# Even stage unrolled over heads, with chunk scores and turned keys computed once, decay rows brought by DMA, and four attention weights loaded into buffers of their own

## The reference

```python
b = lax.cumsum(fc, axis=2)
d = jnp.where(lower, b[..., :, None] - b[..., None, :] + ic[..., None, :], -jnp.inf)
inter = b + m_st[..., None]
m_t = jnp.maximum(inter, jnp.max(d, axis=-1))
w = jnp.exp(d - m_t[..., None])
a_inter = jnp.exp(inter - m_t)
s = jnp.einsum('bhtd,bhsd->bhts', qc, kc) * w
num = jnp.einsum('bhts,bhsd->bhtd', s, vc) + a_inter[..., None] * jnp.einsum('bhtk,bhkd->bhtd', qc, c_st)
den = jnp.sum(s, axis=-1) + a_inter * jnp.einsum('bhtk,bhk->bht', qc, n_st)
h = num / jnp.maximum(jnp.abs(den), jnp.exp(-m_t))[..., None]
...
kw = kc * w_tok[..., None]
c_new = decay[..., None, None] * c_st + jnp.einsum('bhsk,bhsd->bhkd', kw, vc)
n_new = decay[..., None] * n_st + jnp.sum(kw, axis=2)
```

## Time and profile before

| | us |
|---|---|
| median of 3 runs | 3407.57 (3403.55 to 3410.09) |
| the profiled execution | 3409.28 |
| its span, first to last instruction | 3407.5 |
| PE busy | 3097.1 (91%) |
| DVE busy | 1566.3 (46%) |
| ACT busy | 1215.2 (36%) |

### The profile page before, as it was taken

The page is one execution under the profiler, slowest core; times in us unless marked ns, Lnnn a source line. Parts: engine busy times, 40 slices in busy tenths (PEclk is TensorE's granted clock), DMA queues, the critical chain, the costliest instruction groups (busy, mean ns, idle before and its releaser), DMA issues. The chain is left out here.

```text
span 3407.5 us, 42438 instructions
## 1 busy us (share of the span) xinstructions
PE 3097.1 (91%) x16797; PEld 2659.2 (78%) x16797; DVE 1566.3 (46%) x2651; ACT 1215.2 (36%) x1967; POOL 102.1 (3%) x118
## 2 busy tenths in 40 slices
PE   5547999999999999999799799699999999999798
PEld 4436898888888888888678578588888888888577
DVE  3352354235424542454444332265665665665443
ACT  2331222122212221222221432166666666665400
POOL 0000000000000000000023000000000000000000
PEclk7768999999999999999899899899999999999899
DMA  5401111111111101110533323100000000000431
GB/s 186 148 26 39 32 33 33 49 31 33 33 54 32 33 27 54 31 33 29 211 100 104 127 68 99 54 23 22 26 29 29 26 29 31 18 29 19 161 99 62
DMA packets 217411, 196.27 MB, mean 58 GB/s; under 512 B 10350, under 2 KB 191998, under 8 KB 217218
## 3 DMA queue, kind: packets, MB, share of 16 engines
q1 hardware_dynamic: 200916, 166.82, 15.5%
q0 software_dynamic: 5904, 21.50, 1.7%
q10 hardware_dynamic: 10400, 5.24, 0.5%
HBM read 152.62 MB, written 40.91 MB: 57 GB/s over the span
## 5 line engine op out<-in xcount | busy, mean ns | idle before, releaser
L40 PE MATMUL v_pj<-e_u_hi,v_w_hi 128*128 128x512 f32 (+1 forms) x1728 | 624.4, 361 | 18.8 <-issue 9.7
L41 PE MATMUL v_pj<-e_u_lo,v_w_hi 128*128 128x512 f32 (+1 forms) x1728 | 620.7, 359 | 0.9 <-issue 0.9
L42 PE MATMUL v_pj<-e_u_hi,v_w_lo 128*128 128x512 f32 (+1 forms) x1728 | 620.6, 359 | 0.0
L40 PEld LDWEIGHTS v_pj<-e_u_hi,v_w_hi 128*128 128x128 f32 x1728 | 329.8, 191 | 66.7 <-issue 19.6
L42 PEld LDWEIGHTS v_pj<-e_u_hi,v_w_lo 128*128 128x128 f32 x1728 | 329.3, 191 | 52.3 <-issue 1.1
L41 PEld LDWEIGHTS v_pj<-e_u_lo,v_w_hi 128*128 128x128 f32 x1728 | 329.7, 191 | 46.9
L40 PE MATMUL o_y_bank<-o_w_hi,o_m_hi 128*128 128x512 f32 x576 | 230.8, 401 | 48.0 <-DVE o_w_lo L1083 31.2
L1670 ACT CAST t_pt_hi<-t_ring 128x512 fp32r<-128x512 f32 (+1 forms) x384 | 181.3, 517 | 253.7 <-PE t_ring L1853 253.7
L41 PE MATMUL o_y_bank<-o_w_lo,o_m_hi 128*128 128x512 f32 x576 | 228.9, 397 | 0.0
L42 PE MATMUL o_y_bank<-o_w_hi,o_m_lo 128*128 128x512 f32 x576 | 228.7, 397 | 0.0
L1768 DVE TENSOR_REDUCE t_bias<-t_scores 128x1 f32<-128x1280 f32 x128 | 190.8, 1490 | 81.2 <-PE t_scores L1879 80.6
(11 more groups left out here) (335 smaller groups left out, 6093.5 us busy)
## 6 DMA issues: line engine op xcount, KB each, us to landing
v_w_raw<-in_ev_w_in SPq DMA_DIRECT2D x73, 512.0 KB, 3.8
m_w_raw<-in_mod_w SPq DMA_DIRECT2D x24, 1024.0 KB, 5.7
l_w_raw<-in_od_w_in SPq DMA_DIRECT2D x21, 512.0 KB, 3.8
o_m_raw<-mixT SPq DMA_DIRECT2D x20, 512.0 KB, 4.8
mixT<-v_buf SPq DMA_DIRECT2D x16, 512.0 KB, 2.7
o_w_raw<-in_ev_w_out SPq DMA_DIRECT2D x16, 512.0 KB, 9.5
zgT<-l_lat_q POOLq DMA_DIRECT2D x16, 512.0 KB, 3.4
t_zg<-zgT SPq DMA_DIRECT2D x32, 256.0 KB, 2.7
```

The source lines that it names most:

```text
L40: nc.tensor.matmul(out, whi, xhi, start=first, stop=False)
L41: nc.tensor.matmul(out, whi, xlo, start=False, stop=False)
L42: return nc.tensor.matmul(out, wlo, xhi, start=False, stop=last)
```

## The change

`stage_gates` writes the R rows of all heads and directions to a small tensor in memory. `stage_even` loses its loops: every engine's program is written out for 4 heads of 18 tiles. The scores and the turned keys of a chunk are made once for both directions, between the projections of tiles 4 and 5 (`prepare`), and VectorE copies them into SBUF over the halves of k. The decay rows come by a DMA that spreads a row over 128 partitions, two steps ahead, and GpSimd adds the mask. Z takes v with its column of ones (258 columns), so Y_n and its four short matmuls go. The waits are split: Y, Z and X have semaphores of their own. The convolution weights of all heads are loaded at once at the start of the stage. In `stage_attend` the first four weight loads have four buffers, laid over a tensor that is written later, and are issued one after the other without waiting.

```diff
+            sp.wait_ge(logf, 6)
+            for d in range(2):
+                sp.dma_start(a["r_rows"][4 * d:4 * d + 4, :], rows2("R")[32 * d:32 * d + 4, :]).then_inc(row_out, 16)
+            sp.wait_ge(row_out, 32)
...
+    PREPARED = {(4, 0): (0, 1), (4, 1): (2, 3), (4, 2): (4, 5), (5, 0): (6, 7), (5, 2): (8, 9)}
...
+        k_tok = over(nc, "v_k_tok", [P, 2, NT, P], F32, k_hi_at)
+        s_all = over(nc, "v_s_all", [P, NT, P], F32, k_lo_at)
...
+        wgt = [[s.sb(f"wgt{d}{x}", [P, P]) for x in range(2)] for d in range(2)]
...
+        Z = z_bank[:, :].rearrange("p (j c) -> p j c", c=512)[:, :, 0:HD + 2]
+        prep_bank = lambda c: e_bank[:, :] if c % 2 == 0 else z_half[1]
...
+            def load_row(h, n, d):
+                c = chunk(n, d)
+                old = step_at[(h, n, d)] - 4
+                if old > 0:
+                    sp.wait_ge(sw_ok, old)
+                row = a["r_rows"][4 * d + h:4 * d + h + 1, c * P:c * P + P]
+                sp.dma_start(wgt[d][n % 2][:, :], row.partition_broadcast(P)).then_inc(rows_in[d][n % 2], 16)
...
+            sp.dma_start(conv_w[:, :, :], a["conv_t"].rearrange("(m p) w -> p m w", p=P)).then_inc(cw_in, 16)
+            for d in range(2):
+                for n in range(2):
+                    load_row(0, n, d)
+            for h, t in tiles:
+                if tile_no[(h, t)] + 1 < len(tiles):
+                    load_w(*tiles[tile_no[(h, t)] + 1])
+                n = step_of(t)
+                if n is not None:
+                    nxt = (h, n + 2) if n + 2 < NT else (h + 1, n + 2 - NT)
+                    if nxt[0] < HEADS:
+                        for d in range(2):
+                            load_row(*nxt, d)
+                if t == 10:
+                    store(h, 1, 2 * h, (gate_part, gate_at[(h, 9, 2)]))
+                if t == 14:
+                    store(h, 1, 2 * h + 1, (gate_part, gate_at[(h, 13, 2)]))
+                if t == NTILE - 1:
+                    for j in range(2):
+                        store(h, j, KD + 2 * h + j, (ht_used, ht_at[(h, j, 2)]))
+            sp.wait_ge(mix_out, 32 * len(stores))
...
+        def _(pool):
+            pool.wait_ge(const_ok, 1)
+            for h, n, d in steps:
+                x = n % 2
+                pool.wait_ge(rows_in[d][x], 16 * (h * (NT // 2) + n // 2 + 1))
+                pool.tensor_tensor(wgt[d][x][:, :], wgt[d][x][:, :], mask[:, d, :], ALU.add).then_inc(masked, 1)
...
+                act.wait_ge(masked, g)
+                wg = wgt[d][n % 2]
+                nc.scalar.activation(wg[:, :], wg[:, :], ACT.Exp, bias=gate_col[:, 0, c, col:col + 1]).then_inc(wgt_ok, 1)
+                act.wait_ge(prep_ok, prep_at[(h, NT - 1)])
+                if g > 2:
+                    act.wait_ge(x_done, g - 2)
+                nc.scalar.mul(kw[d][0][:, :].rearrange("p (j e) -> p j e", e=P), k_tok[:, :, c, :], gate_col[:, 3, c, col:col + 1]).then_inc(kw_hi_ok, 1)
...
+            def prepared(h, c):
+                dve.wait_ge(prep_done, prep_at[(h, c)])
+                bank = prep_bank(c)
+                nc.vector.tensor_copy(s_all[:, c, :], bank[:, 0:P])
+                nc.vector.tensor_copy(k_tok[:, :, c, :], bank[:, P:3 * P].rearrange("p (j e) -> p j e", e=P)).then_inc(prep_ok, 1)
...
+                nc.vector.tensor_tensor(wg[:, :], s_all[:, c, :], wg[:, :], ALU.mult).then_inc(sw_f_ok, 1)
-                nc.vector.tensor_tensor(wgt[d][:, :], sek[d][:, 0:P], wgt[d][:, :], ALU.mult).then_inc(sw_f_ok, 1)
-                nc.vector.scalar_tensor_tensor(kw[d][1][:, :], sek[d][:, 2 * P:4 * P], hc[:, 3, c, d:d + 1], f(kw[d][0][:, :]),
+                parts = lambda ap: ap.rearrange("p (j e) -> p j e", e=P)
+                nc.vector.scalar_tensor_tensor(parts(kw[d][1][:, :]), k_tok[:, :, c, :], gate_col[:, 3, c, col:col + 1], parts(f(kw[d][0][:, :])),
...
+                    dve.wait_ge(z_done, with_state[st])
-                        nc.vector.tensor_copy(c_f32[d][:, :, HD:HD + 2], Y_n)
-                        nc.vector.tensor_copy(c_f32[d][:, :, 0:HD], Z).then_inc(c_f_ok, 1)
+                        nc.vector.tensor_copy(c_f32[d][:, :, :], Z).then_inc(c_f_ok, 1)
-                        dve.wait_ge(inter_ok, i * (NSTEP - 2) + 2 * (n - 1) + d + 1)
-                        for dst, new in ((slice(HD, HD + 2), Y_n), (slice(0, HD), Z)):
-                            last = nc.vector.scalar_tensor_tensor(c_f32[d][:, :, dst], c_f32[d][:, :, dst], hc[:, 5, c, d:d + 1],
-                                                                  new, ALU.mult, ALU.add)
-                        last.then_inc(c_f_ok, 1)
-                else:
-                    dve.wait_ge(inter_ok, i * (NSTEP - 2) + 2 * (n - 1) + d + 1)
+                        nc.vector.scalar_tensor_tensor(c_f32[d][:, :, :], c_f32[d][:, :, :], gate_col[:, 5, c, col:col + 1],
+                                                       Z, ALU.mult, ALU.add).then_inc(c_f_ok, 1)
...
-            def scores(i, n, d):
-                c = n if d == 0 else BWD[n]
-                t0 = c * P
-                if n == 0:
-                    pe.wait_ge(ht_used, i * 6 + 1)
-                    pe.wait_ge(pj_free_d, i * (3 * len(D_TILES)) + 13)
-                pe.wait_ge(diag_ok, i * NSTEP + 2 * n + d + 1)
-                bank = sek[d]
+            def prepare(h, c):
+                t0, bank = c * P, prep_bank(c)
+                pe.wait_ge(pj_free_d, dve_free[(h, 3, group_of(c))])
+                if c >= 2:
+                    pe.wait_ge(prep_ok, prep_at[(h, c - 2)])
+                elif h:
+                    pe.wait_ge(ht_used, ht_at[(h - 1, 1, 2)])
-                nc.tensor.matmul(bank[:, P:2 * P], ones[:, :], diag[d][:, :], start=True, stop=False)
-                nc.tensor.matmul(bank[:, P:2 * P], ident_b[:, :], mask[:, d, :], start=False, stop=True)
-                    nc.tensor.matmul(bank[:, (2 + j) * P:(3 + j) * P], k_hi[:, j, t0:t0 + P], ident_r[:, :], start=True, stop=False)
-                    last = nc.tensor.matmul(bank[:, (2 + j) * P:(3 + j) * P], k_lo[:, j, t0:t0 + P], ident_r[:, :], start=False, stop=True)
-                last.then_inc(sc_done, 1)
-            def state(i, n, d):
-                c, g = (n if d == 0 else BWD[n]), 2 * n + d
-                t0 = c * P
+                    nc.tensor.matmul(bank[:, (1 + j) * P:(2 + j) * P], k_hi[:, j, t0:t0 + P], ident_r[:, :], start=True, stop=False)
+                    last = nc.tensor.matmul(bank[:, (1 + j) * P:(2 + j) * P], k_lo[:, j, t0:t0 + P], ident_r[:, :], start=False, stop=True)
+                last.then_inc(prep_done, 1)
...
-                    pe.wait_ge(vt_ok, i * 6 + 6)
-                pe.wait_ge(step_ok, i * NSTEP + g + 1)
-                pe.wait_ge(num_ok, i * NSTEP + g + 1)
+                    pe.wait_ge(vt_ok, vt_at[(h, 1, 2)])
+                    pe.wait_ge(prep_ok, prep_at[(h, NT - 1)])
+                    if prev in with_inter:
+                        pe.wait_ge(inter_ok, with_inter[prev])
+                    pe.wait_ge(c_ok, with_state[(h, n - 1, d)])
-                pe.wait_ge(kw_lo_ok, i * NSTEP + g + 1)
+                    last.then_inc(y_done, 1)
+                    pe.wait_ge(kw_lo_ok, g)
+                    if prev in with_state:
+                        pe.wait_ge(c_f_ok, with_state[prev])
-                        mm3(nc, Z[:, j, :], (kw[d][0][:, kj], kw[d][1][:, kj]), (v_hi[:, c, 0:HD], v_lo[:, c, 0:HD]))
-                        nc.tensor.matmul(Y_n[:, j, :], kw[d][0][:, kj], ones_r[:, :], start=True, stop=False)
-                        nc.tensor.matmul(Y_n[:, j, :], kw[d][1][:, kj], ones_r[:, :], start=False, stop=True)
-                pe.wait_ge(sw_ok, i * NSTEP + g + 1)
-                mm3(nc, X, (sw[d][0][:, :], sw[d][1][:, :]), (v_hi[:, c, :], v_lo[:, c, :])).then_inc(st_done, 1)
...
+                        last = mm3(nc, Z[:, j, :], (kw[d][0][:, kj], kw[d][1][:, kj]), (v_hi[:, c, :], v_lo[:, c, :]))
+                    last.then_inc(z_done, 1)
+                pe.wait_ge(sw_ok, g)
+                if prev:
+                    pe.wait_ge(num_ok, step_at[prev])
+                mm3(nc, X, (sw[d][0][:, :], sw[d][1][:, :]), (v_hi[:, c, :], v_lo[:, c, :])).then_inc(x_done, 1)
...
+            for h, t in tiles:
+                n = step_of(t)
+                pe.wait_ge(w_ok, tile_no[(h, t)] + 1)
+                for j in range(3):
+                    project(h, t, j)
+                    for c in PREPARED.get((t, j), ()):
+                        prepare(h, c)
+                    if t in (5, 6) and j == 1:
+                        v_transposes(h, t - 5)
+                    if n is not None and j:
+                        state(h, n, j - 1)
+                if t == NTILE - 1:
+                    pe.wait_ge(h_ok, step_at[(h, NT - 1, 1)])
+                    for j in range(2):
+                        for g, (c0, nch) in enumerate(VGROUPS):
+                            if (j, g) == (1, 2):
```

(77 more changed lines are left out.)

495 lines of the change are left out of this document (198 added, 297 removed).

## The result

The changed kernel takes 3275.29 us (median of four runs, 3274.38 to 3280.84); the kernel before, on the same chip, 3405.56 (four runs, 3401.47 to 3410.09). The ratio is 0.9621, with a 95% interval of 0.9603 to 0.9638. The forecast was 3283 us in a range of 3270 to 3312.

The account below looks back on a forecast made before the run. TensorE, busy 91% of the span, was taken as the bound. Terms of -69, -31.7, -17, +1.5, +2 and -10.3 sum to -124.5 from 3409.3: 3284.8, with the median 1.7 lower, 3283 us; range 3270 to 3312.

Parts of the forecast that it names:

- Scores and turned keys, -69: Even layer: two scores blocks per step go, 114.0 us; 40 prepare blocks of 1.13 us add 45; net -69 us.
- Y_n, -31.7: Even-layer states: four short matmuls and the restart behind them cost 0.44 us, 72 times; removing them gives -31.7 us.
- Loops, -17: Starts of heads 1 to 3: 3.33 us gap plus 2.41 us slow matmuls vanish when loops are written out; -17 us.
- the third case: Head boundaries: the 3.3 us gaps could be the engine's set-up rather than the branch's, and stay.
- rival 2: Head boundaries or attention start keep their gaps: +17 or +5 us, 3288 to 3305 us; chance 0.14.
- VectorE behind the taps, +1.5: Eight tiles behind convolution taps: X waits 0.2 to 0.5 us for VectorE after tile 7, nothing after tile 11; +1.5 us.
- Decay rows, mask, 0: Step tiles: row loads and GpSimd's mask adds, estimated 0.3 us each, hide beside TensorE; zero, bounds 0 and 5 us.
- The prediction's row against the rule on the shared port: GpSimd's add at 2202.61 ran beside a 0.69 us VectorE instruction, not lengthened by its size, despite the port-lock rule.
- Start, +2: Even layer's start: mask queues behind first weights, engines wait for all convolution weights; +2 us, bounds 0 and 6.
- Attention start, -10.3: Before the first query projection: the 8.69 us gap and slow start behind it go; -10.3 us, bounds -5 and -11.

Follow-up runs that it names:

- the run with the third gap filled: Against the one with two gaps closed: in the attention stage, head 1's third key projection moved from slot 4 to slot 1, into a TensorE wait; 3268.3 us.
- the one with two gaps closed: Against the changed kernel: first weights split before mask and constants; next head's first projection put into the wait among the closing transposes; 3269.62 us.

## Why the prediction was right

The step tiles, the boundaries and the attention start are where it put the time; each part that was made or undone alone is worth about what its term says.

- **Scores and turned keys, -69.** Two `scores` blocks out of 40 tiles, 114 us, is right. The 40 `prepare` blocks add 10.9 us per head, 1.09 each, against 1.13: -70.
- **Y_n, -31.7.** Head 1, from the second group of v's transposes to the first closing ones, took 230.95 us before and 194.42 after. Of the 36.53 us, ten tiles' scores are 28.5; 8.03 are left for 18 states, -32 in all. Put back they cost 30.75.
- **Loops, -17.** Heads 1 to 3 became 31.5 us shorter on average, of which 25.5 are in the head: 6.0 per boundary, -17.9; alone, -16.7. The Trainium skill ("Runtime: NRT & Kernel Launch", Instruction fetch mechanics) lays such a stop to a taken branch, and the trace agrees: without the branch it is gone. The set-up of the engine, which the prediction calls the third case and lists as rival 2, fell. Both instruction queues moved 2.42 MB, 62 bytes for each of 39024 instructions, about the 64 of before. Head 0, without a boundary, gained 0.75 us more than this sum. It lies in its first 24 matmuls, behind the wait for the first weights: 5.21 us before and 4.41 after, with the clock at its lower level until 289 us before and until 288 after. So it is the clock's and not work taken away: this tile takes 16.3 to 16.4 us in the three profiles of kernels with the old start, and 15.5 to 15.7 in all with the new one but that of three row loads.
- **VectorE behind the taps, +1.5.** Tile 8 takes 0.15 us more than its neighbours, 0.6 us in all; tile 12 takes nothing more, as the prediction's text has it, though its term counts eight tiles. The mechanism is that of the prediction, at the very edge: in tile 8 Z as well as X just touches VectorE, neither waits. One late instruction of 1.4 us was paid there in full, in tile 12 for the most part, and nowhere else.
- **Decay rows, mask, 0.** GpSimd's 80 adds of 128 columns took 0.43 us each in the median and 0.98 at most, where the estimate was 0.3; nothing waits for them. The prediction's row against the rule on the shared port ("SBUF — State Buffer" of the Trainium skill, engine ports) was no test of it, since that VectorE instruction reads t_ring, a PSUM bank. The kernel after does test it, and the trace agrees with the rule (last section). But the adds meet other instructions than the weighing, so that it costs no time: with 0.6 us behind the taps in all, an effect there can't be told from zero. Row loads land in 3.1 us in the median, weights in 4.7 instead of 3.8; both have room, the weights least behind tiles 8 and 12, where the cast came 7.1 us after the issue at the earliest (2.3 to spare by these medians, not 6).
- **Start, +2.** Measured +1.7.
- **Attention start, -10.3.** Measured -11.15, and -10.9 alone.
- **Not in the sum:** -1.1 in the gates stage, which is within what executions differ by (in the twelve profiles the even layer's first load is issued at 270.6 to 277.0 us), and -4.1 in the rest of the attention stage, which isn't the change's but luck of this profile. The kernel before with and without parts of the change, and six variants of the kernel after, show 992 us there; the profile of the kernel after, and that with `prepare` twice, 988.

In the profiles the terms give -124.5 and the difference is -134.9: 3.6 us more in the heads, 0.9 at the boundaries, 0.9 at the attention start, 0.3 at the start, 1.1 and 4.1 from outside, less 0.6 in other stages, up to rounding. The first four make 5.7, close to the 5.8 us by which the medians fell beyond the forecast.

## What to carry to other kernels

Count TensorE's instructions before its columns where blocks are small: a matmul of two columns cost 0.107 us here and one of 128 columns 0.11, so folding a narrow product into a neighbour's extra columns is nearly free time. Before taking work from the bound engine, compute the start of the next operand from the other engines' timeline, tile by tile: the room was over 3 us in most step tiles, 0.5 in four and nothing in four, and a delay of 1.4 us was paid in these eight alone. And a loop's way back over a few heads cost 5.6 to 6 us each, 3.3 of gap and the rest slow clock behind it.

## What the hardware showed that I had not expected

- Behind one and the same wait of 3.3 us TensorE's clock fell in nine of eleven executions and stayed up in two, with 2.5 to 3.2 us between them. (The rest of the 4.1 us arises near the end of the stage, where the clock fell some 919 us behind the first scores in the nine and in the run with the third gap filled, and not in the two.) The stretch behind the wait, in the kernel after and in the one with two gaps closed:

```profile
2090.00:2094.00 4.00, 2.64 (x12) 2.20 (x13) 1.76 (x4) 2.90 (x4) 0.00 (x0) 1.00 0.00 0
```
```profile
2083.90:2087.90 4.00, 2.62 (x6) 2.14 (x7) 1.78 (x4) 2.92 (x4) 0.00 (x0) 0.52 0.00 0
```

  Twelve matmuls against six in the same four microseconds. An eighth of a per cent between two single profiles can be just this.
- The length of a wait doesn't settle it either. In the run with three row loads TensorE waits 1.67, 2.12 and 1.69 us in tile 15 of heads 0, 2 and 3. Behind the first two the clock stayed at 1.00; behind the third it fell:

```profile
1489.20 0.39 PE L40 MATMUL v_z<-v_vv_hi,v_kw_hi 128*128 128x258 f32 x1 [1.69 <-DVE v_kw_lo L757]
```
```profile
1490.00:1492.00 2.00, 2.00 (x9) 1.71 (x8) 1.90 (x4) 0.55 (x2) 0.00 (x0) 0.59 0.53 158
```
- GpSimd and VectorE do hold each other up. Nine of the 80 adds of the kernel after began while VectorE ran line 710 or 714, whose two operands both lie in SBUF. These nine took 0.64 to 0.98 us, and each ended 0.3 us after VectorE's instruction did; the other 71 took 0.42 to 0.43, also those beside lines 702 and 707, which read PSUM. Twice the add began first: then it took 0.43 us, and VectorE's line 710 took 0.91 and 0.94 instead of 0.69. One pair of each kind, in tiles 9 and 13 of head 1:

```profile
744.19 0.69 DVE L710 SCALAR_TENSOR_TENSOR v_buf<-v_buf 128x512 f32<-128x512 f32 x1
744.25 0.92 POOL L556 TENSOR_TENSOR v_wgt<-v_wgt,v_mask 128x128 f32<-128x128 f32 x1 [0.38 <-DMA v_wgt<-r_rows]
```
```profile
814.75 0.43 POOL L556 TENSOR_TENSOR v_wgt<-v_wgt,v_mask 128x128 f32<-128x128 f32 x1 [0.40 <-DMA v_wgt<-r_rows]
814.82 0.91 DVE L710 SCALAR_TENSOR_TENSOR v_buf<-v_buf 128x512 f32<-128x512 f32 x1
```
- Loads that spread a row over 128 partitions move slowly. In the kernel with three of them per direction, 740 to 800 us in 40 slices, the stretches of row loads show 26 to 52 GB/s, while the 512 KB weight loads reach 187 to 359:

```profile
GB/s 0 0 0 42 44 49 28 52 42 187 185 0 0 0 0 42 41 44 26 43 31 99 267 30 5 0 0 15 44 43 30 39 43 46 359 348 94 0 0 0
```
